# Sample attention on four column groups of the array, stacked rotary parts, head splits on ScalarE and GpSimd

## The chip, the core and the metric

The kernel runs on one core of a Trainium2 chip. The metric is the device time of one launch in microseconds. Engines are TensorE (PE; its weight loads are shown apart as PEld), VectorE (DVE), ScalarE (ACT), GpSimd (POOL) and SyncE (SP), which here only issues transfers.

## What is computed

One inference step of a decoder layer for a prompt of 512 tokens and a sample group of 8 sequences with 4 new tokens each. The part that the change touches is multi-head latent attention with 8 heads. In the prompt each head has its own keys (128 latent dimensions and 64 rotary ones shared by all heads). The sample attends to 2048 past positions in a paged cache of latent rows and to its own new tokens; its queries are absorbed into the latent space first, so all 8 heads and 4 tokens of a sequence make 32 query columns against one set of latent rows:

```python
s_past = einsum('bqhr,bkr->bhqk', q_abs, past_c) + einsum('bqhd,bkd->bhqk', q_pe, past_pe)
s_new  = einsum('bqhr,bkr->bhqk', q_abs, kv_c) + einsum('bqhd,bkd->bhqk', q_pe, k_pe)
s = concatenate([s_past, s_new], -1) * MLA_SCALE
p = softmax(where(visible, s, -inf))
o = einsum('bhqk,bkr->bqhr', p[..., :P], past_c) + einsum('bhqk,bkr->bqhr', p[..., P:], kv_c)
```

Around it stand the input projection, a gated MLP, the output projection, attention to a memory and a squared-ReLU MLP.

## The kernel before

The kernel is written engine by engine, with counting semaphores; nothing reorders it. Weights come as a stream of units of 512 KB through four raw buffers (RAW). ScalarE makes the high part of a unit (w_hi), GpSimd the low part (w_lo, line 344), and TensorE uses both: a product in split precision is three passes (PASSES: high-high, high-low, low-high) in float32r. The parts of the sample are plain float32.

The stage of the change is a loop of 8 rounds (TensorE lines 1393 to 1449). Round h does head h of the prompt and sequence b = h of the sample. TensorE's order in a round:

1. scores of the sample, four quarters of 512 positions: each two products with 128 rows (L1406) and one with the 64 rotary rows (L1407), all into partitions 0 to 31 of two PSUM banks in turn; ScalarE copies a quarter to SBUF (quarter_out, L520), VectorE takes its maximum (quarter_max, L945);
2. scores of the new keys (L1410, L1411);
3. transposes of the prompt's probabilities (L1416), then the values of the prompt (L1426), which wait for the split of these probabilities (L536 on ScalarE, L983 on VectorE);
4. seventeen small transposes of the sample's probabilities (L1431 to L1435), after an exponential over 2080 columns on 32 partitions (L539);
5. values of the sample, 16 pages and the new rows (L1440, L1441);
6. scores of the prompt's next head (head_scores, L1386 with 128 rows, L1389 with 64 rotary rows);
7. the sample's latent output turned into columns (L1447), stored by VectorE (L1000).

VectorE also splits the next head's queries, rotary queries, keys and values (stage_qk, L902 and L906; stage_v, L911 and L912) and adds the squares of the head's output (L996, L997). GpSimd is idle from the weight splits before the loop to those after it.

SyncE, in each round: read 16 page numbers into registers (L309), issue 16 transfers of page columns (L317, 192 KB each, into KT[0] to KT[3], each quarter free after its scores, kt_used), then, when the sample's values of the round before are done (pvs), 16 of page rows (L323, 128 KB each, into NAT). KT[2] and KT[3] lie over raw weight buffers. After the loop it loads weight units again.

Of the kernel before, what the change touches and what calls it, by code (L numbers as in the profile page):

```python
# [25 lines left out]
P = 128  # L26
# [9 lines left out]
QUART = PAGES // 4  # L36
MEM, MH = 256, 4
# [43 lines left out]
N_CONST = C_NEW + NB * NS  # L81
# [22 lines left out]
def trunk(nc, w_stream, x_t, mem_t, gains, consts, w_sp_t, w_sp_4, b_sp, w_uk_t, w_uv_p, pool_t, pool_n,  # L104
          pages, mem_k_t, mem_v_p, y_t, kv_t, pe_t, mk_t, mv_p, cv_t):
    with ExitStack() as ctx:
# [20 lines left out]
        def sem(name):  # L127
# [8 lines left out]
        ACCA = place("head_square_sum", [P, TOK], F32, ARENA + 13312)  # L136
        S_AT = at_end[0]
        RX = fixed("rstd_x", [P, TOK])
        TMP = [fixed(f"square{s}", [P, TOK]) for s in range(2)]
        ACC = fixed("square_sum", [P, TOK])  # L140

        S = place("sample_scores", [NS, PAST + NS], F32, S_AT)
        assert S_AT + (PAST + NS) * 4 <= at_end[0]
# [4 lines left out]
        PES = fixed("k_rope_sample", [ROPE, NS])  # L148
        KNAT = fixed("latent_sample_rows", [NS, RT * 128])
# [5 lines left out]
        QR = fixed("q_rope_batch", [ROPE, NS])  # L155
        SMX = fixed("sample_quarter_max", [NS, 8])
        SM = fixed("sample_max", [NS, 1])
        SB = fixed("sample_bias", [NS, 1])
        SS = fixed("sample_sum", [NS, 1])
        SR = fixed("sample_rsum", [NS, 1])  # L160
        PNT = fixed("new_probs_t", [NS, NS])
# [31 lines left out]

        KT = [place(f"page_cols{q}", [P, QUART, 384], F32, at)
              for q, at in enumerate((TB, TB + 6144, ARENA, ARENA + 6144))]
        QH = place("q_head_split", [P, 2, NP], F32R, TB + 12288)
        QRH = place("q_rope_head_split", [P, 2, NP], F32R, TB + 16384)
        KH = place("k_head_split", [P, 2, NP], F32R, TB + 20480)
        VH = place("v_head_split", [P, 2, 4, 128], F32R, TB + 24576)
        NAT = place("page_rows", [P, PAGES, 256], F32, TB + 28672)  # L200
        PTH = []
        off = 45056
# [3 lines left out]
        PST = place("sample_probs_t", [P, PAGES, NS], F32, TB + 56320)  # L206
        SO = place("sample_latent_rows", [NS, RT * 128], F32, ARENA + 12288)
# [26 lines left out]
        def first_bank(g):  # L234
# [11 lines left out]
        ld_kt = [sem(f"loaded_page_cols{q}") for q in range(4)]  # L246
# [15 lines left out]
        stg_qk, stg_v, sc, nb, ex, pn = [  # L262
            sem(n) for n in ("head_qk_staged head_v_staged head_scored head_bias_ready head_exp "
                             "head_probs_ready").split()]
        pt, pt_hi, pt_lo, pv, h_out = [sem(n) for n in "probs_t probs_t_hi probs_t_lo head_valued head_out".split()]
        qst, kt_used, s_max, s_out, sn, s_bias, sex, s_t, pst, pvs, s_rows, s_cols, ol = [
            sem(n) for n in ("sample_q_staged quarter_scored quarter_max quarter_out new_keys_scored "
                             "sample_bias_ready sample_exp sample_probs_transposed sample_probs_t_ready sample_valued "
# [20 lines left out]
        def _(sp):  # L289
# [47 lines left out]
        @block.gpsimd  # L337
        def _(pool):
            pool.sem_inc(w_lo, 4)

            with pool.Fori(0, UNITS // 4) as i:
                for s in range(4):
                    pool.wait_ge(w_hi, i * 4 + (s + 1))
                    nc.gpsimd.tensor_tensor(HL[s % 2][:, 1, :, :], RAW[:, s, :, :], HL[s % 2][:, 0, :, :].bitcast(F32),  # L344
                                            ALU.subtract).then_inc(w_lo, 1)

        @block.scalar
        def _(act):
            act.sem_inc(fsq, 1)
            act.sem_inc(pst, 1)  # L350
# [160 lines left out]

            act.wait_ge(c_n, 8)
            with act.Fori(0, HEADS // 2) as i:
                for hp in range(2):
                    h = i * 2 + hp

                    def quarter_out(q):

                        act.wait_ge(kt_used, h * 4 + (q + 5))
                        nc.scalar.copy(S[:, 512 * q:512 * q + 512], PSUM[0:NS, 4 + q % 2, :]).then_inc(s_out, 1)  # L520

                    quarter_out(0)
                    act.wait_ge(nb, h + 1)
                    for qb in range(4):
# [1225 lines left out]
```

## Time and profile before

| | |
|---|---|
| runs | 2740.46, 2752.51 and 2753.41 us |
| median | 2752.51 us |
| span of the profiled execution, first to last instruction | 2727.6 us |
| TensorE matmuls busy | 2575.2 us, 94% |
| weight loads | 2402.3 us, 88% |
| VectorE, ScalarE, GpSimd busy | 34%, 23%, 34% |
| mean granted TensorE clock | 0.975 |
| attention loop (first sample scores to last latent columns) | 497.3 to 764.7 us |

Times in the rows are from the start of the span, in us. An engine's busy time counts its instructions, not its waits; register instructions of SyncE are not counted. Matmul ends are modelled, so starts are the better measure. The time around the span is not in the profile.

### The profile page before, as it was taken

The page shows a single profiled execution, that of the slowest core. Times are in us where ns is not written, and L with a number is a line of the kernel's source. Part 1 is how long each engine was busy: PE and PEld are TensorE (multiplying, and loading weights), DVE is VectorE, ACT ScalarE, POOL GpSimd, SP SyncE. Part 2 cuts the span into 40 slices and gives each one's busy share as a digit, 9 for nine tenths or more (in the row PEclk, how much of TensorE's full clock was granted, in tenths as well). Part 3 has the DMA queues.
Part 4 walks back from the last instruction along what each step waited for, and adds up shares of the span by engine and source line. Part 5 has one row for each costly group of instructions (what it writes and reads, how often), then busy time and mean ns, then how long its engine had stood idle before and what let it go on. Part 6 is the DMA issues. An engine that isn't in the chain of part 4 may idle for free.

```text
span 2727.6 us, 48074 instructions
## 1 busy us (share of the span) xinstructions
PE 2575.2 (94%) x19084; PEld 2402.3 (88%) x19084; DVE 937.0 (34%) x1260; ACT 633.8 (23%) x855; POOL 919.2 (34%) x380
## 2 busy tenths in 40 slices
PE   7999878999989996999999999999999999999996
PEld 7999867444479995899999999999999999999996
DVE  5200497555443344652122131131131221221356
ACT  5111431222221132132122121121221221221221
POOL 2433432000014441233433434344343433434342
PEclk9999989899989998999999999999999999999998
DMA  5222232455432224122222222222222222222222
GB/s 220 85 85 92 93 121 70 146 155 170 145 133 87 85 78 154 40 77 92 85 86 91 85 92 85 89 88 85 92 85 91 86 86 91 85 92 85 88 89 88
DMA packets 100269, 270.68 MB, mean 99 GB/s; under 512 B 11810, under 2 KB 48707, under 8 KB 99075
## 3 DMA queue, kind: packets, MB, share of 16 engines
q1 hardware_dynamic: 92160, 243.57, 26.8%
q10 hardware_dynamic: 8066, 26.53, 2.6%
q8 instruction: 29, 0.48, 0.1%
q14 instruction: 14, 0.11, 0.0%
HBM read 263.72 MB, written 6.33 MB: 99 GB/s over the span
## 4 chain that ended last, share of the span: by engine, by line
PE 59%; issue 29%; POOL 8%; DVE 3%; ACT 1%; ACTq 0%; POOLq 0%; DVEq 0%
PE psum L1200 58%; POOL hl L344 8%; DVE square L1040 1%; DVE square_sum L1042 1%; DVE x L1037 0%; PE psum L1523 0%; DVE x L1187 0%; ACTq L603 0%; PE psum L1564 0%; ACT mem_probs L621 0%; PE psum L1502 0%; DVE mem_probs L1115 0%; PE psum L1537 0%; DVE head_max L1100 0%; DVE rstd_x L703 0%
## 5 line engine op out<-in xcount | busy, mean ns | idle before, releaser
L344 POOL TENSOR_TENSOR hl<-raw,hl 128x1024 fp32r<-128x1024 f32 x376 | 919.0, 2445 | 1777.5 <-ACT hl L651 913.1
L1200 PE MATMUL psum<-xg,hl 128*128 128x272 f32 x10272 | 1301.4, 289 | 33.5 <-DVE xg L698 20.3
L1200 PEld LDWEIGHTS psum<-xg,hl 128*128 128x128 f32 x10272 | 1297.5, 190 | 36.4 <-POOL hl L344 22.4
L1200 PE MATMUL psum<-ffn_hidden,hl 128*128 128x272 f32 x6144 | 765.9, 287 | 0.0
L1200 PEld LDWEIGHTS psum<-ffn_hidden,hl 128*128 128x128 f32 x6144 | 765.1, 188 | 0.0
L651 ACT CAST hl<-raw 128x1024 fp32r<-128x1024 f32 x254 | 267.7, 1054 | 1209.0 <-PE psum L1200 1209.0
L1175 DVE TENSOR_TENSOR x<-x,psum 128x544 f32 x112 | 80.9, 722 | 561.1 <-PE psum L1200 561.1
L1160 DVE SCALAR_TENSOR_TENSOR square<-psum,rstd_x 128x544 f32<-128x544 f32 x64 | 46.4, 725 | 486.2 <-PE psum L1200 486.2
L1164 DVE TENSOR_SCALAR ffn_hidden<-square 128x544 f32 x64 | 132.4, 2069 | 60.9 <-ACT square L660 60.9
L373 ACT CAST hl<-raw 128x1024 fp32r<-128x1024 f32 x64 | 67.4, 1053 | 318.6 <-PE psum L1200 318.6
L366 ACT CAST hl<-raw 128x1024 fp32r<-128x1024 f32 x58 | 60.6, 1048 | 188.6 <-PE psum L1200 136.6
L1042 DVE TENSOR_TENSOR square_sum<-square_sum,square 128x544 f32<-128x544 f32 x48 | 99.2, 2066 | 1.7
L1037 DVE TENSOR_TENSOR x<-x,psum 128x544 f32 x48 | 34.6, 722 | 151.7 <-PE psum L1200 144.0
L736 DVE TENSOR_TENSOR z<-psum,rstd_x 128x544 f32 x18 | 13.1, 725 | 199.7 <-PE psum L1200 199.7
L1440 PE MATMUL psum<-page_rows,sample_probs_t 128*32 128x256 f32 x256 | 65.1, 419 | 6.6 <-ACT new_probs_t L543 6.6
L1440 PEld LDWEIGHTS psum<-page_rows,sample_probs_t 128*32 128x32 f32 x256 | 30.2, 120 | 38.7 <-issue 17.6
L1406 PE MATMUL psum<-page_cols,q_abs_batch 128*32 128x512 f32 x128 | 62.6, 613 | 0.0
L520 ACT COPY sample_scores<-psum 32x512 f32<-32x512 f32 x32 | 18.4, 575 | 165.8 <-PE psum L1407 165.8
L1200 PE MATMUL psum<-mem_out_split,hl 128*128 128x272 f32 x384 | 50.9, 294 | 2.8 <-DVE mem_out_split L1143 1.9
L1200 PEld LDWEIGHTS psum<-mem_out_split,hl 128*128 128x128 f32 x384 | 49.8, 194 | 3.8 <-issue 3.8
L1166 DVE TENSOR_TENSOR ffn_hidden<-square,ffn_hidden 128x544 f32 x64 | 46.4, 726 | 12.8 <-DVE ffn_hidden L1164 7.6
L1406 PEld LDWEIGHTS psum<-page_cols,q_abs_batch 128*32 128x32 f32 x128 | 11.6, 110 | 42.4 <-issue 42.1
(218 smaller groups left out, 1344.7 us busy)
## 6 DMA issues: line engine op xcount, KB each, us to landing
raw<-in_w_stream SPq DMA_DIRECT2D x376, 512.0 KB, 3.3
page_cols<-in_pool_t SPq DMA_DIRECT2D x128, 192.0 KB, 3.6
page_rows<-in_pool_n SPq DMA_DIRECT2D x128, 128.0 KB, 2.4
x<-in_x_t ACTq DMA_DIRECT2D x4, 1088.0 KB, 12.3
out<-x SPq DMA_DIRECT2D x8, 544.0 KB, 2.7
cache_k_sb<-in_mem_k_t ACTq DMA_DIRECT2D x4, 1024.0 KB, 13.2
cache_v_sb<-in_mem_v_p ACTq DMA_DIRECT2D x1, 4096.0 KB, 19.2
x<-in_x_t ACTq DMA_DIRECT2D x1, 4080.0 KB, 14.1
```

The lines of the kernel that those rows point to most:

```text
L344: nc.gpsimd.tensor_tensor(HL[s % 2][:, 1, :, :], RAW[:, s, :, :], HL[s % 2][:, 0, :, :].bitcast(F32), ALU.subtract).then_inc(w_lo, 1)
L366: nc.scalar.copy(HL[n % 2][:, 0, :, :], RAW[:, n % 4, :, :]).then_inc(w_hi, 1)
L373: nc.scalar.copy(HL[n % 2][:, 0, :, :], RAW[:, n % 4, :, :]).then_inc(w_hi, 1)
L651: nc.scalar.copy(HL[n % 2][:, 0, :, :], RAW[:, n % 4, :, :]).then_inc(w_hi, 1)
L1042: step(tt(a0, a0, t0, ALU.add))
L1160: stt(two(TMP[0][:, :]), banks(g), 0.0, two(RX[:, :]), ALU.max, ALU.mult).then_inc(t_out, 1)
L1164: ts(hh, hs, 1.0, None, ALU.mult).then_inc(h_parts, 1)
L1166: tt(H[:, 1, bass.ds(p * 2 + t, 1), :], hs, hh.bitcast(F32), ALU.subtract).then_inc(h_parts, 1)
L1175: tt(xs, xs, banks(g), ALU.add).then_inc(t_out, 1)
L1200: last = mm(PSUM[:, s + half, 0:HALF], HL[slot][:, wp, blk, :], src[:, xp, k, HALF * half:HALF * (half + 1)], start=start and n == 0, stop ...
L1406: mm(dst, QA[:, r, :], KT[q][:, :, 128 * r:128 * r + 128], start=r == 0, stop=False)
L1440: mm(PSUM[0:NS, 7, 0:256], PST[:, g, :], NAT[:, g, :], start=g == 0, stop=False)
```

## The change

- Page columns KT become one buffer with 320 columns a page (128 + 128 latent, and the 64 rotary dimensions of two halves of 64 positions on 128 partitions) instead of 384; page rows NAT now lie over the raw weight buffers.
- The sample's scores go to one PSUM bank: quarter q on partitions 32q to 32q+31, so each quarter is a column group of the array; the rotary part is two products per quarter with 128 rows, of which 64 meet zeros. Softmax is done on 128 partitions at once with one exponential (S4), the new keys apart (SN). The probabilities are turned by four full transposes. Values are four products per group. Quarters are added when the output is turned into columns, by a matrix C_SUM4 in place of the identity, and division by the sum comes last (latent_out).
- Rotary queries are stacked: high part of one half and low part of the other on 128 rows (QRT against the high keys, QRZ against the low), five products per block in place of six.
- Splits: high parts on ScalarE (stage_qk_hi, stage_v_hi), low parts on GpSimd (stage_qk_lo, stage_v_lo). ScalarE copies the head's output and squares it, GpSimd adds the squares.
- Order on TensorE: scores of the sample, new keys, transposes of sample and prompt, values of the sample, scores of the next head, values of the prompt, columns. The scores of a ninth head are no longer computed.
- All loops over heads are written out; SyncE reads page numbers at constant places.

```diff
-            with sp.Fori(0, NB) as b:
-                pages_of = [sp.value_load(PTAB[0:1, bass.ds(b * PAGES + g, 1)], min_val=0,
+            for b in range(NB):
+                pages_of = [sp.value_load(PTAB[0:1, b * PAGES + g:b * PAGES + g + 1], min_val=0,
                                           max_val=pool_n.shape[0] - 1) for g in range(PAGES)]
-                for q in range(4):
-                    sp.wait_ge(kt_used, b * 4 + (q + 1))
-                    if q == 2:
-                        sp.wait_ge(w_lo, U_OUT + 2 + 4)
-                    for g in range(QUART):
-                        sp.dma_start(KT[q][:, g, :], pool_t[bass.ds(pages_of[QUART * q + g], 1), :, :]
-                                     .rearrange("a p n -> (a p) n")).then_inc(ld_kt[q], 16)
-                sp.wait_ge(w_used, U_KV)
-                sp.wait_ge(pvs, b + 1)
+                if b:
+                    sp.wait_ge(kt_used, b)
+                for g in range(PAGES):
+                    sp.dma_start(KT[:, g, :], pool_t[bass.ds(pages_of[g], 1), :, :]
+                                 .rearrange("a p n -> (a p) n")).then_inc(ld_kt, 16)
+                if b:
+                    sp.wait_ge(pvs, b)
+                else:
+                    sp.wait_ge(w_lo, U_OUT + 2 + 4)
                 for g in range(PAGES):
                     sp.dma_start(NAT[:, g, :], pool_n[bass.ds(pages_of[g], 1), :, :]
                                  .rearrange("a p n -> (a p) n")).then_inc(ld_nat, 16)
-            sp.wait_ge(kt_used, 4 * NB + 4)
+            sp.wait_ge(pvs, NB)
             load_unit(U_OUT + 2, 2, U_OUT + 3)
-            sp.wait_ge(s_cols, NB)
-            sp.wait_ge(stat_sum, STAT_NO["a"] + 1)
             load_unit(U_OUT + 3, 3, U_OUT + 4)
...
+            def stage_qk_lo(h):
+                pool.wait_ge(qk_hi, h + 1)
+                for dst, src in ((QH, Q[:, h, 0:NP]), (KH, KK[:, h, :])):
+                    last = nc.gpsimd.tensor_tensor(dst[:, 1, :], src, dst[:, 0, :].bitcast(F32), ALU.subtract)
+                last.then_inc(stg_qk, 1)
+            def stage_v_lo(h):
+                pool.wait_ge(v_hi, h + 1)
+                nc.gpsimd.tensor_tensor(VH[:, 1, :, :], VV[:, :, 128 * h:128 * h + 128],
+                                        VH[:, 0, :, :].bitcast(F32), ALU.subtract).then_inc(stg_v, 1)
+            stage_qk_lo(0)
+            stage_v_lo(0)
+            for h in range(HEADS):
+                if h + 1 < HEADS:
+                    stage_qk_lo(h + 1)
+                pool.wait_ge(h_out, h + 1)
...
+                    nc.gpsimd.tensor_tensor(ACCA[:, 0:NP], ACCA[:, 0:NP], HSQ[:, :], ALU.add).then_inc(hsum, 1)
...
+                if h + 1 < HEADS:
+                    stage_v_lo(h + 1)
...
+            for h in range(HEADS):
+                if h + 1 < HEADS:
+                    stage_qk_hi(h + 1)
+                if h:
+                    act.wait_ge(pv, h)
+                    nc.scalar.copy(Q[:, h - 1, 0:NP], PSUM[:, 6, :])
+                    if h > 1:
+                        act.wait_ge(hsum, h - 1)
+                    nc.scalar.activation(HSQ[:, :], PSUM[:, 6, :], ACT.Square).then_inc(h_out, 1)
+                    stage_v_hi(h)
+                act.wait_ge(nb, h + 1)
...
+                act.wait_ge(s_bias, h + 1)
+                nc.scalar.activation(S4[:, :], PSUM[:, 4, :], ACT.Exp, bias=SB[:, :], scale=MLA_SCALE,
+                                     accum_out=SS[:, :])
+                nc.scalar.activation(SN[:, :], SN[:, :], ACT.Exp, bias=SB[0:NS, :], scale=MLA_SCALE,
+                                     accum_out=SSN[:, :]).then_inc(sex, 1)
+                act.wait_ge(s_t, h + 1)
+                nc.scalar.copy(PNT[0:NS, :], PSUM[0:NS, 7, 448:448 + NS])
+                nc.scalar.copy(PST[:, :, :], PSUM[:, 5, :].rearrange("p (g q) -> p g q", g=QUART)).then_inc(pst, 1)
...
+                dve.wait_ge(kt_used, h + 1)
+                step(nc.vector.reduce_max(SMQ[:, :], PSUM[:, 4, :], AX))
+                for q in range(4):
+                    nc.vector.tensor_copy(SMX[:, q:q + 1], SMQ[NS * q:NS * q + NS, :])
+                dve.wait_ge(sn, h + 1)
+                step(tt(SN[:, :], PSUM[0:NS, 7, 256:256 + NS], C[0:NS, C_NEW + NS * h:C_NEW + NS * h + NS], ALU.add))
+                step(nc.vector.reduce_max(SMX[:, 4:5], SN[:, :], AX))
+                step(nc.vector.reduce_max(SM[:, :], SMX[:, 0:5], AX))
+                for q in range(4):
+                    last = ts(SB[NS * q:NS * q + NS, :], SM[:, :], -MLA_SCALE, None, ALU.mult)
+                last.then_inc(s_bias, 1)
...
+            for h in range(HEADS):
+                pe.wait_ge(qst, h + 1)
+                pe.wait_ge(ld_kt, (h + 1) * (16 * PAGES))
+                for r in range(RT):
                     for q in range(4):
+                        mm(PSUM[NS * q:NS * q + NS, 4, :], QA[:, r, :],
+                           KT[:, QUART * q:QUART * q + QUART, 128 * r:128 * r + 128], start=r == 0, stop=False)
+                for half in range(2):
+                    for q in range(4):
+                        dst = PSUM[NS * q:NS * q + NS, 4, :].rearrange("p (g k) -> p g k", g=QUART)
+                        last = mm(dst[:, :, 64 * half:64 * half + 64], QR[:, half, :],
+                                  KT[:, QUART * q:QUART * q + QUART, 256:PAGE_W], start=False, stop=half == 1)
+                last.then_inc(kt_used, 1)
...
+                pe.wait_ge(pst, h + 1)
+                pe.wait_ge(ld_nat, (h + 1) * (16 * PAGES))
+                for g in range(QUART):
+                    for q in range(4):
+                        mm(PSUM[NS * q:NS * q + NS, 7, 0:256], PST[:, g, NS * q:NS * q + NS],
+                           NAT[:, QUART * q + g, :], start=g == 0, stop=g == QUART - 1 and q > 0)
+                mm(PSUM[0:NS, 7, 0:256], PNT[:, :], KNAT[:, :], start=False, stop=True).then_inc(pvs, 1)
+                pe.wait_ge(pt_lo, h * 4 + 4)
+                if h + 1 < HEADS:
+                    head_scores(h + 1)
...
+                pe.wait_ge(stg_v, h + 1)
...
+                last.then_inc(pv, 1)
+                pe.wait_ge(s_rows, h + 1)
+                pe.wait_ge(s_sum, h + 1)
+                for r in range(RT):
+                    mm(PSUM[:, 7, 320 + 32 * r:352 + 32 * r], SO[:, 128 * r:128 * r + 128],
+                       C[:, C_SUM4:C_SUM4 + NS], start=True, stop=True)
...
```

## Rows read from the trace of the kernel before

**Rows 1.** Stretches table: us, busy PE, PEld, DVE, ACT, POOL; clock, DMA share, GB/s.

```profile
592.00:623.00 31.00, 28.85 (x129) 13.54 (x128) 15.90 (x43) 9.67 (x21) 0.00 (x0) 1.00 0.53 164
```

**Rows 2.** Timeline of one head, TensorE: start, us, engine, line, tiles, count.

```profile
593.03 0.62 PE L1386 MATMUL psum<-k_head_split,q_head_split 128*128 128x256 f32 x3
...
598.45 0.63 PE L1447 MATMUL psum<-consts_sb,sample_latent_rows 32*128 32x32 f32 x4
...
599.00 1.90 PE L1406 MATMUL psum<-page_cols,q_abs_batch 128*32 128x512 f32 x4
...
599.46 0.11 PEld L1406 LDWEIGHTS psum<-page_cols,q_abs_batch 128*32 128x32 f32 x1 [0.32 <-issue]
...
599.88 0.11 PEld L1406 LDWEIGHTS psum<-page_cols,q_abs_batch 128*32 128x32 f32 x1 [0.32 <-issue]
...
610.23 0.31 PE L1410 MATMUL psum<-latent_sample,q_abs_batch 128*32 128x32 f32 x4
...
610.64 1.31 PE L1416 MATMUL psum<-consts_sb,probs 128*128 128x128 f32 x10
...
613.29 2.18 PE L1426 MATMUL psum<-probs_t,v_head_split 128*128 128x512 f32 x12 [1.33 <-DVE probs_t L983]
...
617.58 7.09 PE L1440 MATMUL psum<-page_rows,sample_probs_t 128*32 128x256 f32 x32 [0.82 <-ACT new_probs_t L543]
...
625.14 0.62 PE L1386 MATMUL psum<-k_head_split,q_head_split 128*128 128x256 f32 x3
```

**Rows 3.** SyncE: transfers in the timeline, reads by line (ns), landing, waits.

```profile
593.27 8.08 SPq L323 DMA_DIRECT2D page_rows<-in_pool_n  x16
...
612.33 8.35 SPq L317 DMA_DIRECT2D page_cols<-in_pool_t  x16
...
L309 SPq FUSED_REGOPS  x248: 46/152/173, 452.6 to 709.8; - x124
...
L309 SPq TENSOR_LOAD <-page_ids x128: 261/263/463, 452.1 to 709.6; - x128
...
page_cols<-in_pool_t SPq DMA_DIRECT2D x128, 192.0 KB, 3.6
...
SPq L323 <- PE psum L1441: 32.1, 7, 6.1
```

**Rows 4.** Timeline of the same head, VectorE and ScalarE.

```profile
602.52 0.67 DVE L945 TENSOR_REDUCE sample_quarter_max<-sample_scores 32x1 f32<-32x512 f32 x1 [0.18 <-ACT sample_scores L520]
...
603.76 0.68 ACT L526 ACTIVATE probs<-psum,head_bias 128x512 f32<-128x512 f32 x1
...
604.33 0.20 ACT L526 ACTIVATION_READ_ACCUMULATOR probs<-psum,head_bias 128x1 f32 x1
...
611.55 0.17 DVE L972 TENSOR_TENSOR sample_scores<-psum,consts_sb 32x32 f32<-32x32 f32 x1
...
612.47 1.67 DVE L983 TENSOR_TENSOR probs_t<-psum,probs_t 128x512 fp32r<-128x512 f32 x4
```

**Rows 5.** Splits on GpSimd, and an addition on VectorE (by group, in the timeline).

```profile
L344 POOL TENSOR_TENSOR hl<-raw,hl 128x1024 fp32r<-128x1024 f32 x376 | 919.0, 2445 | 1777.5 <-ACT hl L651 913.1
...
L1042 DVE TENSOR_TENSOR square_sum<-square_sum,square 128x544 f32<-128x544 f32 x48 | 99.2, 2066 | 1.7
...
594.43 0.69 DVE L997 TENSOR_TENSOR head_square_sum<-head_square_sum,probs 128x512 f32<-128x512 f32 x1
```

**Rows 6.** Timeline ahead of the loop.

```profile
487.91 1.01 PE L1386 MATMUL psum<-k_head_split,q_head_split 128*128 128x256 f32 x3 [1.75 <-DVE q_abs_sample L925]
...
489.45 4.69 POOL L344 TENSOR_TENSOR hl<-raw,hl 128x1024 fp32r<-128x1024 f32 x2 [16.48 <-ACT hl L366]
...
497.32 3.62 PE L1406 MATMUL psum<-page_cols,q_abs_batch 128*32 128x512 f32 x4
```

**Rows 7.** Timeline of the last head.

```profile
749.37 8.78 PE L1440 MATMUL psum<-page_rows,sample_probs_t 128*32 128x256 f32 x32 [0.82 <-ACT new_probs_t L543]
...
764.02 0.63 PE L1447 MATMUL psum<-consts_sb,sample_latent_rows 32*128 32x32 f32 x4
```

More of the change, by code:

```diff
@@ L36 @@
 QUART = PAGES // 4
+PAGE_W = 320
 MEM, MH = 256, 4
@@ L80 @@
 C_NEW = C_BLOCK + NS
-N_CONST = C_NEW + NB * NS
+C_SUM4 = C_NEW + NB * NS
+N_CONST = C_SUM4 + NS
 class Chain:
@@ L192, in trunk @@
         PR = place("probs", [P, 1280], F32, TB + 96320)
[L194 to L200, printed above, removed]
+        KT = place("page_cols", [P, PAGES, PAGE_W], F32, TB)
+        QH = place("q_head_split", [P, 2, NP], F32R, TB + 20480)
+        QRT = place("q_rope_stack", [P, NP], F32R, TB + 24576)
+        QRZ = [place(f"q_rope_hi{s}", [P, NP], F32R, TB + 26624 + 2048 * s) for s in range(2)]
+        KH = place("k_head_split", [P, 2, NP], F32R, TB + 30720)
+        VH = place("v_head_split", [P, 2, 4, 128], F32R, TB + 34816)
         PTH = []
-        off = 45056
+        off = 38912
         for kb, w in enumerate((512, 384, 256, 256)):
@@ L245, in trunk @@
         ld_w = [sem(f"loaded_unit_slot{s}") for s in range(4)]
-        ld_kt = [sem(f"loaded_page_cols{q}") for q in range(4)]
+        ld_kt = sem("loaded_page_cols")
         ld_nat = sem("loaded_page_rows")
@@ L923, in _ @@
+            for s in range(2):
+                nc.vector.memset(QRZ[s][ROPE * (1 - s):ROPE * (1 - s) + ROPE, :].bitcast(F32), 0.0)
+            stage_rope(0)
+            nc.vector.memset(QR[:, :, :], 0.0)
+            nc.vector.memset(PNT[:, :], 0.0)
+            nc.vector.memset(PTH[3][:, 0, 0:128].bitcast(F32), 0.0)
+            step(nc.vector.memset(PTH[3][:, 1, 0:128].bitcast(F32), 0.0))
             for r in range(RT):
@@ new lines, in _ @@
+            for h in range(HEADS):
+                dve.wait_ge(sc, h + 17)
+                for qb in range(4):
+                    d = PSUM[:, qb, 128 * qb:128 * qb + 128]
+                    last = tt(d, d, causal, ALU.add)
+                step(last)
+                for qb in range(4):
+                    last = nc.vector.reduce_max(HM[:, qb:qb + 1], PSUM[:, qb, 0:128 * (qb + 1)], AX)
+                step(last)
+                ts(HN[:, :], HM[:, :], -MLA_SCALE, None, ALU.mult).then_inc(nb, 1)
+                if h:
+                    latent_out(h - 1)
+                dve.wait_ge(kt_used, h + 1)
[9 more added lines that the diff above has]
+                last.then_inc(s_bias, 1)
+                dve.wait_ge(ex, h + 1)
+                step(nc.vector.reciprocal(HR[:, :], HS[:, :]))
+                for qb in range(4):
+                    p_ = PR[:, P_AT[qb]:P_AT[qb] + 128 * (qb + 1)]
+                    last = ts(p_, p_, HR[:, qb:qb + 1], None, ALU.mult)
+                last.then_inc(pn, 1)
+                dve.wait_ge(sex, h + 1)
+                step(tt(SS[0:NS, :], SS[0:NS, :], SSN[:, :], ALU.add))
+                ts(SSB[:, :], ones, SS[:, :], None, ALU.mult).then_inc(s_sum, 1)
+                if h + 1 < HEADS:
+                    stage_rope(h + 1)
+                    stage_sample(h + 1)
+                for kb in range(4):
+                    dve.wait_ge(pt_hi, h * 4 + (kb + 1))
+                    lo = 0 if kb < 3 else 128
+                    w = NP - 128 * kb
+                    tt(PTH[kb][:, 1, lo:lo + w], PSUM[:, kb, 128 * kb:NP],
+                       PTH[kb][:, 0, lo:lo + w].bitcast(F32), ALU.subtract).then_inc(pt_lo, 1)
@@ L1376, in _, with head_scores @@
             pe.wait_ge(t_out, G_KV + 16)
[L1379 to L1382 removed]
+            def head_scores(h):
+                pe.wait_ge(stg_qk, h + 1)
+                pe.wait_ge(stg_r, h + 1)
                 for qb in range(4):
                     w = max(256, 128 * (qb + 1))
+                    q = slice(128 * qb, 128 * qb + 128)
                     for n3, (qp, kp) in enumerate(PASSES):
[L1386 to L1391 removed]
```

337 lines of the change are left out of this document (133 added, 204 removed).

## The prediction

> **What bounds the kernel now.** I read the table of stretches first. In the stage that the change touches, the eight heads of attention, TensorE is busy 28.85 of 31 us, VectorE 15.9 and every other engine less [rows 1]. So the stage is a TensorE stage, and its period is read from the timeline of one head: the score products of the next head start at 593.03 and again at 625.14, so one head takes 32.11 us [rows 2]. Within it: scores of the prompt 5.42 us (593.03 to 598.45), the columns of the sample's latent output 0.55, scores of the sample against its pages 11.23 (599.00 to 610.23), the new keys 0.41, transposes of the prompt's probabilities 1.31, values of the prompt 2.18, values of the sample 7.09 and 0.5 for the new keys (617.58 to 625.14); the rest is small transposes and two waits of 1.33 and 0.82 us. The sample's scores and values are 18.8 of 32.1 us, and the weight of each of their products has 32 columns out of 128.
>
> Then I read the queue of SyncE, which no line about busy engines shows. Per head it issues 16 transfers of page rows in 8.08 us and 16 of page columns in 8.35 us. Between the end of the one (593.27 + 8.08 = 601.35) and the start of the other (612.33) lie 10.98 us, in which it reads 16 page numbers (128 reads in eight heads) [rows 3]. That is 27.4 us of work per head in strict order. Today it waits 32.1 us in 7 times for the sample's values, 4.6 us a head [rows 3], so it has slack, and little of it: 32.1 - 4.6 = 27.5.
>
> **The change part by part.**
>
> *Sample scores and values on four column groups.* The number of products does not fall: 8 of 512 columns and 8 of 256 for the scores, 16 of 256 for the values. What may fall is the time, if groups run at once. One product is two matmuls: weight loads of one product start at 599.46 and 599.88, 0.43 apart [rows 2]. A product of 256 columns takes 7.09 / 16 = 0.44. One after another the scores are 16 x 0.43 + 8 x 0.44 = 10.4 us and the values 7.0; with four at once 3.0 and 2.0. No row shows two groups side by side, so these are the bounds. I take two at once, 5.6 and 3.7 us: the two matmuls of one product go to the same group one after the other, and if matmuls start in program order, as they do in all these rows, the next group can only overlap the second of them.
> The Trainium skill says the same in "TensorE: Matmul & The Clock Gate" (The mechanism): matmuls to different tiles overlap, but start and end strictly in order. By its 2.38 times for three column tiles the scores would be an estimated 4.4 us. It changes the TensorE period below, not the period that I forecast.
>
> *Stacked rotary parts.* 24 products become 20, all with 128 rows. The 24 take 5.42 us; the 12 products of the prompt's values, which have half as many columns in all and no change of row count, take 2.18 [rows 2]. So the 8 changes of row count cost (5.42 - 4.36) / 8 = 0.13 us each, and 20 products without a change are 2.18 x 20 / 12 = 3.6 us. Bounds 3.6 and 4.5 (20/24 of 5.42).
>
> *The chain between scores and values.* It was partly covered; now nothing of the prompt's values stands in it. After the scores, VectorE reduces all partitions once (0.67) instead of four quarters, does the new keys' part and the maxima, which take 0.9 today from 611.55 to 612.47, and seven tiny operations more (0.17 at most each, overlapping: some 0.9): 2.5 us [rows 4]. ScalarE's exponential of 512 columns with its read of the sum is 0.9 (603.76 to 604.53) and that of the 32 new keys some 0.4 [rows 4]; together TensorE stands 3.8 us after the scores, with 0.4 of new keys beside it. Five full transposes instead of seventeen small ones: 5 x 0.13 = 0.65; ten for the prompt 1.3 [rows 2]. The exponential of 2080 elements on 32 partitions and three ScalarE copies of quarters go.
>
> TensorE's period: 3.6 + 2.2 (values of the prompt) + 0.8 (three products for the columns instead of two, 0.55 x 1.5) + 5.6 + 3.8 + 0.65 + 1.3 + 3.7 + 0.5 + 0.3 for handing over = 22.4 us. One after another it is 30.5, with four at once 18.1. The clock adds to this: values of the sample took 7.09 busy us in the head shown and 8.78 in the last head [rows 2, 7], after the same stretch of transposes and waits, so one fall of the clock costs 1.7 us. The new waits are longer, so I put one or two falls into each head: 24 to 26 us.
>
> *Head splits moved to ScalarE and GpSimd.* A split of 512 columns on GpSimd is half of 2.4 us [rows 5]; two for queries and keys, one for values and one addition of squares are 4.9 us a head, started early in a period of over 20. The first copies and the squares on ScalarE are some 3 us more in a queue that is busy a third of the time. On VectorE they go. VectorE operations with operands in SBUF wait for GpSimd: an addition of 544 columns took 2.07 us beside its weight splits, one of 512 took 0.69 in the loop, where GpSimd is idle [rows 5]. GpSimd's work comes in the first 6 us of a period, where VectorE does the prompt's maximum, not on the chain above. Cost: none; if that cover is gone, 1 us a head.
>
> *SyncE's queue.* The order is read numbers, columns, rows, as before, with 16 reads and 32 transfers per head. The transfers cost what they do, 8.35 + 8.08. The index of a read becomes a constant. A read has two register steps today, the shorter 0.046 us [rows 3]; with the time to issue it I estimate 0.09 us, so at best the 16 reads lose 1.4 us, and the loop's branch goes. At worst they lose nothing. So the queue needs 9.6 + 8.35 + 8.08 + 0.3 = 26.3 us a head, between 25.7 and 27.4. This is longer than TensorE's 22 to 26. All waits in the queue come true earlier than it reaches them, so the stage's period is that of the queue: **26.3 us**.
>
> *Start.* The first head's splits stand behind two weight splits on GpSimd, which end at 489.45 + 4.69 = 494.1 [rows 6], and take 2.4: TensorE starts the first scores at 496.5 instead of 487.9 and, standing idle, at the low clock (three products took 1.01 against 0.62 [rows 2, 6]). The sample's first scores start at about 501.8 instead of 497.3 [rows 6]. That is covered by the queue: page rows of head 0 are issued from 494.3 (they wait for that same weight split), until 502.4; numbers until 512.0; page columns of head 1 until 520.3, landed 3.6 later [rows 3], 523.9. TensorE would be there at about 525.
>
> *End.* The last head computes no scores for a ninth head: 5.42 us of TensorE go, 2.2 of values move there. The weight loads of the output projection start after the sample's values instead of after its scores; the units are needed 15 us later, so this costs nothing.
>
> *The sum.* Columns of head 7 have landed at 523.9 + 6 x 26.3 = 681.7. From there 5.6 + 3.8 + 0.65 + 1.3 + 4.2 + 2.2 + 0.8 = 18.6 us, with two falls of the clock 22, to the last columns of the latent output: 703.7. Before, they ended at 764.02 + 0.63 = 764.7 [rows 7]. All that follows depends on these and is the same. The gain is **61 us**. It is made against the profiled execution, whose span is 2727.6; the runs lie 13 to 26 us above that span. The median of the runs, 2752.5, gives 2691.5 (own range 2685 to 2701 by the queue's 25.7 to 27.4, six times, and 2 us at the end).
>
> **The rivals.**
> *Groups don't overlap*, so that the change does not do what it says: TensorE's 30.5 us is then the period. 8 x 1.6 = 13 us less, 3 less at the end, 4 more at the start: 2740, within 0.5%. For it: no row shows an overlap, and every product here is two full matmuls. Against: it would need different groups to wait for each other.
> *Slower: every change of column group costs what a change of row count costs*, 0.13 us. With 32 changes a head and no overlap the period is 34.7, so 8 x 2.6 + 1 = 22 us more: 2774. It decides from 0.05 us per change on, where 32 changes eat up the 1.6 us. For it: the measured price of the row changes. Against: the weight shape stays the same from group to group.
> The Trainium skill, "TensorEngine Tiling (Array Packing)" (Key Properties), says that a change of tiling mode drains the array and a change of tile alone does not. The 0.13 us agrees with its first half; on the second half no run here has spoken. By it this rival would not occur; by the first half applied to every group it is the 2774.
> *The queue is not the bound*, because reads with a constant index cost far less than today's 10.98 / 16 = 0.69 us. Then TensorE's 23 to 24 us set the period: some 20 us less than forecast, 2670. Nothing in the rows shows such a read.
>
> **How the numbers follow.** Forecast 0.66, no overlap 0.16, slower 0.10, queue cheap 0.08. Differences under 0.5% (14 us) can't be told from no change here. Faster are the forecast and the cheap queue: 0.74; same is the rival without overlap: 0.16; slower 0.10. The range reaches to the cheap queue and the case without overlap, 2668 to 2741, and leaves out about 2 in 10.
>
> **What would show it.** In the profile after: a head's period of 26 us; SyncE issuing with no wait for TensorE, and TensorE waiting some us before the sample's scores for page columns; about 9.6 us between the last page rows of one head and the first page columns of the next; starts of the sample's matmuls that overlap in pairs, scores 5 to 6 us; 20 score products in 3.6 us; values of the sample slower in many heads by the clock. A period near 30.5 with serial matmuls, or over 32, makes the forecast wrong; so does a queue that still waits.

## The result and the profile after

The changed kernel takes 2653.7 us (median; 2651.6 to 2654.7), the kernel before, run beside it, 2749.8: a ratio of 0.967, 95% interval 0.964 to 0.970, or 96 us less. The forecast was 2691.5 with a range of 2668 to 2741: faster as foretold, but 38 us lower than forecast and 14 below the range.

| us in the profiled execution | before | after | forecast |
|---|---|---|---|
| span | 2727.6 | 2652.9 | 2666.6 (61 less) |
| last columns of the latent output end | 764.7 | 693.6 | 703.7 |
| from there to the end | 1962.9 | 1959.3 | the same |
| period of a head, mean of six | 32.95 (32.1 or 33.8) | 25.8 | 26.3 |
| TensorE waits for page columns | 0 | 33.3 in 7 | some us a head |

The timeline of one head after the change, all engines (SPq is SyncE's queue; the brackets give the idle time ahead and what ended it):

```profile
558.47 2.42 PE L1474 MATMUL psum<-page_rows,sample_probs_t 128*32 128x256 f32 x28
...
560.69 8.06 SPq L324 DMA_DIRECT2D page_cols<-in_pool_t  x16
...
561.24 0.62 PE L1432 MATMUL psum<-k_head_split,q_head_split 128*128 128x256 f32 x3
...
564.55 2.11 PE L1488 MATMUL psum<-probs_t,v_head_split 128*128 128x512 f32 x12
...
568.93 8.43 SPq L332 DMA_DIRECT2D page_rows<-in_pool_n  x16
...
571.92 3.64 PE L1444 MATMUL psum<-page_cols,q_abs_batch 128*32 128x512 f32 x16 [4.67 <-DMA page_cols<-in_pool_t]
...
575.31 1.90 PE L1449 MATMUL psum<-page_cols,q_rope_batch 128*32 128x256 f32 x16
...
581.00 0.23 PE L1459 MATMUL psum<-consts_sb,sample_new_probs 32*32 32x32 f32 x1 [3.62 <-ACT sample_new_probs L595]
...
584.34 3.35 PE L1474 MATMUL psum<-page_rows,sample_probs_t 128*32 128x256 f32 x32
...
586.36 1.88 SPq L324 DMA_DIRECT2D page_cols<-in_pool_t  x4
```

From one issue of page columns to the next is 586.36 - 560.69 = 25.67 us: 8.06 and 8.43 us of issues with 0.18 between them, and from 568.93 + 8.43 = 577.36 to 586.36 the reads of 16 page numbers. TensorE reaches the sample's scores, finds the page columns not landed and waits 4.67 us. The score products that follow run at the lower of the clock's two levels (granted clock 0.50, which is 1.2 GHz, from 571.92 to 575.31): they take 3.64 us, and 1.92 where TensorE didn't wait (below). The prompt's 20 score products take 564.55 - 561.24 = 3.31 us.

The table of stretches there (columns as in [rows 1]):

```profile
550.00:575.00 25.00, 16.70 (x129) 11.47 (x121) 11.00 (x41) 8.43 (x24) 4.95 (x4) 0.77 0.60 181
```

TensorE, 28.85 of 31 us busy before, is busy 16.70 of 25, and its granted clock is 0.77 of full speed in the mean.

Who waits for whom in the eight heads, TensorE and SyncE's queue (us in all, times, longest):

```profile
PE psum L1444 <- DMA page_cols<-in_pool_t: 33.3, 7, 6.9
PE psum L1459 <- ACT sample_new_probs L595: 29.9, 8, 4.6
PE psum L1432 <- POOL k_head_split L365: 11.4, 1, 11.4
...
SPq L332 <- POOL hl L351: 25.4, 1, 25.4
SPq L302 <- PE psum L1476: 10.0, 1, 10.0
```

SyncE waits ahead of the first page rows and behind the last, and nowhere between. Its 32.1 us of waits for the sample's values [rows 3] have gone, and TensorE waits instead.

### The profile page after: what moved, and what is told of

Same layout as the page of the kernel before. It is cut to its first block, busy times and chain, and to the rows that moved or that the text cites. A ratio compares the mean times of both kernels' runs of the same rounds, so it can differ in the third digit from the quotient of the medians.

```text
span 2652.9 us, 47225 instructions
## 1 busy us (share of the span) xinstructions
PE 2447.7 (92%) x19004; PEld 2368.7 (89%) x19004; DVE 893.7 (34%) x1238; ACT 628.7 (24%) x884; POOL 957.4 (36%) x412
## 4 chain that ended last, share of the span: by engine, by line
PE 70%; issue 14%; SPq 5%; POOL 5%; DVE 5%; ACT 1%; ACTq 0%; DVEq 0%; DMA 0%; POOLq 0%
PE psum L1243 67%; POOL hl L351 5%; SPq L318 2%; SPq L324 2%; SPq L332 2%; DVE square L1085 1%; DVE square_sum L1087 1%; PE psum L1394 0%; DVE x L1082 0%; PE psum L1572 0%; DVE x L1232 0%; DVE square L812 0%; PE psum L1613 0%; ACT mem_probs L688 0%; PE psum L1551 0%
## 5 line engine op out<-in xcount | busy, mean ns | idle before, releaser
L382 POOL TENSOR_TENSOR head_square_sum<-head_square_sum,head_square 128x512 f32<-128x512 f32 x7 | 8.8, 1263 | 142.6 <-ACT head_square L581 122.1
L1444 PE MATMUL psum<-page_cols,q_abs_batch 128*32 128x512 f32 x128 | 25.1, 925 | 33.3 <-DMA page_cols<-in_pool_t 33.3
L1243 PE MATMUL psum<-q_split,hl 128*128 128x272 f32 x288 | 40.0, 304 | 4.1 <-DVE q_heads L908 2.9
L1243 PEld LDWEIGHTS psum<-q_split,hl 128*128 128x128 f32 x288 | 39.2, 203 | 5.0 <-DVE q_heads L908 3.3
L1085 DVE TENSOR_TENSOR square<-x 128x544 f32 x48 | 43.1, 897 | 1.6
```

Source lines behind the costliest of these rows:

```text
L1085: step(tt(t0, xs, xs, ALU.mult))
L1243: last = mm(PSUM[:, s + half, 0:HALF], HL[slot][:, wp, blk, :], src[:, xp, k, HALF * half:HALF * (half + 1)], start=start and n == 0, stop ...
```

## The experiments

Ratios are to the kernel before, run on the same chip. Variants of the changed kernel are compared by their medians, since each repeats within 1 to 6 us (but for the shifted one at the end). They did not all run on one chip; from the last columns to the end, where no edit but the shifts reaches, their profiled executions took 1954.5 to 1961.9 us (the changed kernel 1959.3), so differences of 2 or 3 us between variants say nothing.

**What bounds the new kernel: reads at once.** One instruction reads a head's 16 page numbers, without the steps that test their bounds (shortened):

```
-pages_of = [sp.value_load(PTAB[0:1, b * PAGES + g:b * PAGES + g + 1], min_val=0, ...) for g in range(PAGES)]
+pages_of = nc.values_load_multi_w_load_instructions(PTAB[0:1, b * PAGES:(b + 1) * PAGES], ...)[1]
```

> The 16 page numbers of a head are read by one instruction and without the two bounds steps. Theory A, SyncE's queue sets the period of 25.65 us in the changed kernel: the read stretch of 9.3 us shrinks to under 1 us, the queue then needs about 17 us a head, and TensorE's own 20.9 us (25.65 less the mean wait of 33.3 / 7 = 4.76 us for page columns) become the bound. The 33.3 us of waits go: 2653.7 - 33 = about 2620 us, and down to 2608 if the clock, which is low after the waits, recovers. Rival B, the transfers themselves set the period (the DMA engines are 0.60 busy in the loop): issued earlier they land no earlier, the waits for page columns stay, 2645 to 2654.

Measured: 2607.2 us, ratio 0.953 (0.948 to 0.958), 46 less than the changed kernel, as theory A has it with the clock recovered. The reads by line (ns, least/median/most), after and then in this run, and its first waits:

```profile
L318 SPq TENSOR_LOAD <-page_ids x128: 261/266/462, 448.1 to 662.8; - x128
L318 SPq FUSED_REGOPS  x128: 147/147/170, 448.6 to 663.1; - x128
```

```profile
L318 SPq TENSOR_LOAD <-page_ids x8: 967/974/1180, 448.1 to 616.0; - x8
...
PE psum L1460 <- ACT sample_new_probs L596: 30.0, 8, 4.6
PE psum L1433 <- POOL k_head_split L366: 11.4, 1, 11.4
```

The wait for page columns is gone, and the period is 18.7 us. More fell than the 33.3 us of waits: the sample's scores of the eight heads, 32.5 us together in the changed kernel, took 21.0. Without the waits they run at full speed, 1.74 us to the first rotary product against 3.39 above:

```profile
566.78 1.95 PE L1475 MATMUL psum<-page_rows,sample_probs_t 128*32 128x256 f32 x32
...
568.56 0.59 PE L1477 MATMUL psum<-latent_sample_rows,new_probs_t 128*32 128x256 f32 x2
...
575.02 1.92 PE L1445 MATMUL psum<-page_cols,q_abs_batch 128*32 128x512 f32 x16
...
576.76 1.05 PE L1450 MATMUL psum<-page_cols,q_rope_batch 128*32 128x256 f32 x16
...
577.62 0.29 PE L1456 MATMUL psum<-latent_sample,q_abs_batch 128*32 128x32 f32 x4
```

SyncE's queue has little room even so, since its issues of page columns got longer, 9.00 us for 16 against 8.06:

```profile
560.41 9.00 SPq L325 DMA_DIRECT2D page_cols<-in_pool_t  x16
...
560.00:580.00 20.00, 14.53 (x125) 10.91 (x125) 12.55 (x51) 8.46 (x25) 6.82 (x7) 0.91 0.81 248
```

One issue of the 16 takes 1.21 us there, where the others take 0.33; in heads 2 to 7 the longest takes 0.94 to 1.41. The DMA engines are busier over the whole stretch (0.81 instead of 0.60), but while the issues run their share is 0.83 against 0.80, so the share doesn't explain it, and the cause stays open.

**The same edit on the kernel before.**

> The same edit to the kernel before. Theory A, TensorE's 32.1 us a head bounded that kernel and the queue had 4.6 us of slack: SyncE's wait for the sample's values grows from 4.6 to about 14 us a head and the time doesn't move, 2750 within 5 us. Rival B, the queue already limited some heads of the kernel before: faster by 10 us or more.

Measured: 2744.4 us, ratio 1.003 (0.9997 to 1.006): no gain, as theory A has it. SyncE's waits for the sample's values grew from 32.1 us to 93.0 in 7, 13.3 a head, so the time that the reads gave back went into waiting. That queue bounds the kernel after and didn't bound the one before.

**What the column groups are worth.** The group becomes the outer loop, in the scores and in the values (the scores, shortened):

```
-for r in range(RT):                 +for q in range(4):
-    for q in range(4):              +    for r in range(RT):
         mm(PSUM[NS*q:NS*q+NS, 4, :], QA[:, r, :], KT[:, QUART*q:..., 128*r:...], ...)
```

> The changed kernel with the products of one column group issued one after the other (group outermost) in the sample's scores and values; same products, same result. Theory A, matmuls start in the order of the program, so that groups overlap only where neighbours in that order lie in different groups: scores 10 us instead of 2.6, values 6 to 7 instead of 1.8 to 2.7, TensorE 20.9 + 7.6 + 4.5 = 33 us a head, above the queue's 25.65, the waits for page columns go and SyncE waits instead: 2653.7 + 7 x 7.4 + 12 at the end = about 2715 us. Rival B, the four groups run at once whatever the order: 2654. Rival C, half of the overlap stays (5.6 and 3.7 us): TensorE 25.4, hidden under the queue, 2654 to 2660, and the timeline tells it from B.

Measured: 2665.4 us, 12 more than the changed kernel; scores 7.6 us, values 4.2 to 5.6. The period is 26.3 us, just above the queue's 25.8, and TensorE's waits for page columns fall to 1.6 us. The time is near theory C, although less of the overlap stays than C said, and A's premise falls. TensorE in this run:

```profile
603.70 1.90 PE L1444 MATMUL psum<-page_cols,q_abs_batch 128*32 128x512 f32 x4
605.44 0.38 PE L1448 MATMUL psum<-page_cols,q_rope_batch 128*32 128x256 f32 x1
605.45 0.62 PE L1444 MATMUL psum<-page_cols,q_abs_batch 128*32 128x512 f32 x1
605.66 0.59 PE L1448 MATMUL psum<-page_cols,q_rope_batch 128*32 128x256 f32 x2
605.90 0.59 PE L1444 MATMUL psum<-page_cols,q_abs_batch 128*32 128x512 f32 x1
```

A group has four matmuls on L1444 and then four on L1448. The second group's first (605.45) starts beside the first group's fifth (605.44), ahead of its sixth (605.66), which stands earlier in the program. So matmuls of different groups do not start in program order; within a group they do. A reading that fits and was not tested: each group has a queue of its own for a few matmuls. The Trainium skill says in "TensorE: Matmul & The Clock Gate" (The mechanism) that matmuls are strictly first in, first out; this trace differs, and the trace decides.

**The same with reads at once.**

> Page numbers read at once, and the groups issued one after the other. Theory A, TensorE sets the period of 26.3 us of the serial kernel, and taking 8 us of work from the queue changes nothing there: 2660 to 2666, so that the overlap of the groups is worth about 57 us once the queue is out of the way, where it showed as 11 us with the queue in it. Rival B, the queue was still the bound of the serial kernel: 2640 or less.

Measured: 2659.6 us against 2607.2 with the groups interleaved: 52 us, as theory A has it. With the queue in the way the same order cost 12.

**The rotary part taken apart,** with the queue in the way and without (shortened):

```
-mm(.., QRT[:, q], PEH[:, 0, 0:w]);  mm(.., QRZ[h % 2][:, q], PEH[:, 1, 0:w])
+mm(.., QRT[p, q], PEH[p, 0, 0:w]);  mm(.., QRT[p, q], PEH[p, 1, 0:w])
+mm(.., QRZ[1 - h % 2][p, q], PEH[p, 0, 0:w])            # p: 64 rows; VectorE writes the low part there
```

> The changed kernel with the rotary part of the prompt's scores as three products of 64 rows instead of two stacked ones of 128. The 24 products should take 5.4 us again instead of 3.3. Theory A, the queue sets the period: the 2.1 us lie in the wait for page columns, whose sum falls from 33.3 to about 18 us, and the time stays, 2654 within 4 us. Rival B, TensorE sets it: 8 x 2.1 = 17 us more, 2671.

> Page numbers read at once, and the rotary part as three products of 64 rows. Theory A, with the queue out of the way TensorE's 18.7 us set the period, and the 2 us that four times three products of other row count cost now show: 8 x 2 = 16 us more than with the page numbers at once alone, 2607 + 16 = 2623. Rival B, the queue (9 + 8.5 + 1.1 = 18.6 us a head) is still the bound: 2607 to 2612.

Measured: 2657.2 us with the queue in the way (the profiled span is 2653.1, that of the changed kernel 2652.9), and 2624.9 without, 18 more than 2607.2. That is theory A both times. With the queue in the way, the wait for page columns took up the cost; it was 33.3 us and is now:

```profile
PE psum L1446 <- DMA page_cols<-in_pool_t: 22.5, 6, 5.9
```

**Head splits on VectorE again** (second half of each split, heads 1 to 7; reads at once).

> Page numbers read at once, and the second half of the head splits (queries, keys, values) of heads 1 to 7 made by VectorE again instead of GpSimd. A split is 0.69 us on VectorE (an operation of 512 columns) and 1.27 on GpSimd. Theory A, VectorE has room: the two splits of queries and keys stand ahead of the prompt's last subtractions, for which TensorE's next scores wait with about 1.1 us of slack, so the period grows by 0.3 to 1 us: 2609 to 2615 against 2607 with GpSimd. Rival B, hidden wholly: 2605 to 2609, the move to GpSimd is then worth nothing. Rival C, VectorE becomes the chain: 2625 or more.

Measured: 2605.6 us against 2607.2, which can't be told apart: rival B. The move of these to GpSimd is worth nothing here.

**Filling TensorE's wait.** The prompt's values and the columns of the head before go between the sample's scores and its transposes; ScalarE's and VectorE's steps follow. In the second run GpSimd's order is changed too:

```
 for h in range(HEADS):
-    if h + 1 < HEADS: stage_qk_lo(h + 1)
+    if h + 2 < HEADS: stage_qk_lo(h + 2)      # stage_qk_lo(1) ahead of the loop
     pool.wait_ge(h_out, h + 1)
```

> Page numbers read at once, and the prompt's values and the columns of the head before put into TensorE's wait of 3.6 us between the sample's scores and its transposes. TensorE's period would fall from 18.7 to about 16. Theory A, the queue's 18.2 to 18.8 us a head take over at once: 2603 to 2607, no change that can be measured, with waits for page columns back. Rival B, the queue has room: 8 x 2.5 = 20 us less, 2587. Rival C, VectorE's and ScalarE's later steps delay the chain by more than the gap holds: slower than 2612.

> The kernel with the filled wait, with one more edit: GpSimd makes the query and key splits of the head after next before it waits for the squares of the head before, instead of behind that wait. In the run without it TensorE stood 3.1 to 4.7 us before the prompt's scores, six times 23.1 us in all, for a key split that GpSimd had queued behind its wait for ScalarE, and the scores behind it ran at the low clock (5.9 us instead of 3.3). Theory A, that order was the whole reason: TensorE's period falls from 22.25 to about 17, the queue's 18.2 to 18.8 take over, 2603 to 2609. Rival B, the longer way through VectorE and ScalarE was part of it: 2612 to 2620. Rival C, the queue has room and the filled wait pays: 2590.

Measured: 2623.0 and 2608.9 us. The first is rival C, by another way than it said: GpSimd's queue, in strict order, held the next key split behind a wait for ScalarE's squares, and TensorE stood, 23.1 us in six heads. The timeline of one of them:

```profile
573.70 1.28 POOL L383 TENSOR_TENSOR head_square_sum<-head_square_sum,head_square 128x512 f32<-128x512 f32 x1 [16.80 <-ACT head_square L605]
...
576.18 1.26 POOL L366 TENSOR_TENSOR q_head_split<-q_heads,q_head_split 128x512 fp32r<-128x512 f32 x1
577.40 1.26 POOL L366 TENSOR_TENSOR k_head_split<-k_heads,k_head_split 128x512 fp32r<-128x512 f32 x1
578.76 0.98 PE L1433 MATMUL psum<-k_head_split,q_head_split 128*128 128x256 f32 x3 [3.14 <-issue]
```

With the order changed the time is that of reads at once, not 20 us less, since SyncE's queue (18.7 us a head) takes over and TensorE waits for page columns again:

```profile
PE psum L1467 <- DMA page_cols<-in_pool_t: 12.0, 6, 3.2
```

**Sharing the issues.** ScalarE issues four of the 16 transfers of page rows.

> The kernel with the filled wait and GpSimd's new order, in which TensorE waits for page columns again, with one more edit: of the 16 transfers of page rows of heads 1 to 7, ScalarE issues four, with their page numbers, and SyncE twelve. The same bytes move. Theory A, issuing is what limits SyncE's queue: 4 x 0.52 = 2.1 us leave it, the waits for page columns (12.0 us in 6) go, the period falls from 18.7 to about 17.2 and the time from 2609 by 7 x 1.5 = 10 to about 2598. Rival B, the DMA engines' throughput limits it (0.85 busy, 252 GB/s): issues take longer by as much as they get fewer, 2605 to 2610. Rival C, the four issues stand ahead of ScalarE's splits of the next head and delay the chain: 2612 or more.

Measured: 2602.3 us, ratio 0.949 (0.945 to 0.953), the least of all and 6.6 less than without the edit; in the profiled executions 3.5 us of that are in the heads (last columns at 644.0 for 647.5). This is between A and B: the waits for page columns are gone, SyncE waits again,

```profile
SPq L333 <- PE psum L1515: 14.5, 7, 3.2
...
560.00:580.00 20.00, 16.62 (x135) 11.46 (x134) 13.13 (x48) 9.58 (x30) 5.05 (x4) 0.91 0.86 260
580.00:600.00 20.00, 16.62 (x125) 11.01 (x125) 12.55 (x44) 8.69 (x25) 5.07 (x4) 0.83 0.81 246
```

and the period is 18.3 us, TensorE's own, with a granted clock of 0.83 to 0.91. So issuing was the limit, and little lies behind it.

**Why the median of before misled: the same kernel once more, and two shifts in SBUF.**

> The kernel before, unchanged, with another profiled execution. Theory A, the runs of this kernel differ among themselves by what the clock does in the sample's values (6.7 or 8.4 us a head, so up to 8 x 1.7 = 13.5 us) and in the stages behind: the time lies within 2720 to 2755, 1.8 us above its own span, and heads of 32.1 and of 33.8 us alternate in another mixture than the 32.95 us mean of the first profile. Rival B, 13 to 26 us lie around the span in every execution, as the prediction took it: a span near 2727 with a time near 2750.

Measured: the profiled execution took 2751.8 us with a span of 2750.0, so 1.8 us lie around the span, as in every execution on record whose span is known: theory A, B falls. But the clock in the heads, which A named first, doesn't make the 22 us between this span and 2727.6: the heads took 1.9 us longer and started 1.8 earlier, and both executions end the last columns at 764.7. Most of it, 20 us, is in the feed-forward stage (1530.8 and 1551.2 us from its first product to its last), which no edit touches; the granted clock is 1.00 there in both. Mean distance of the starts of its products of 272 columns, worked out from the traces:

| us | input projections (100 to 300) | feed-forward (1280 to 2580) | all runs |
|---|---|---|---|
| before | 0.1261 | 0.1244 | 2740 to 2753, with later runs 2722 to 2754 |
| before again | 0.1250 | 0.1261 | 2728 to 2752 |
| before, shifted | 0.1244 | 0.1244 | 2722 to 2731 |
| after | 0.1244 | 0.1244 | 2652 to 2655 |
| after, shifted | 0.1261 | 0.1256 | 2656 to 2681 |

The change makes some small tiles larger and so moves the region of the activations (TB) from byte 72000 of a partition to 72288. The shifts add unused bytes and nothing else:

```
+fixed("pad", [P, 72])     # before: TB at 72288, as in the changed kernel;  in the changed kernel [P, 56]: TB at 72512
 TB = at_end[0]
```

> The kernel before with 288 unused bytes put ahead of the large region in SBUF that holds the activations, so that this region begins where it begins in the changed kernel (byte 72288 of a partition instead of 72000). No instruction changes. In the three profiled executions of the kernel before, a product of 272 columns in the weight-streaming stages starts every 0.1244, 0.1250, 0.1256 or 0.1261 us, one value for each stage of an execution; in all of the changed kernel and its variants it is 0.1244. 16416 such products times 0.0017 us are 28 us. Theory A, the address sets it: with the region shifted every stage runs at 0.1244 and all runs lie near the lowest of before, 2718 to 2728, within 3 us of each other. Rival B, it hangs on something else that changed, such as the loops of the queues: 2721 to 2753 as before, spread and all.

> The changed kernel with 224 unused bytes at the same place, so that the region begins at byte 72512, on a multiple of 64 as in the kernel before, where the changed kernel has it at 72288, 32 bytes beside one. Theory A, the address sets the rhythm: stages at 0.1250 to 0.1261 us appear, the runs spread over 2655 to 2682. Rival B, it is something else: 2652 to 2656.

Measured: before, shifted, 2727.8 us, ratio 0.9945 (0.9925 to 0.9966); after, shifted, 2674.4 us, 21 more than unshifted. Theory A both ways, although the shifted kernel before spreads over 9 us and not 3. The same 6144 products of the feed-forward stage (busy us, mean ns) in before again, before shifted, after, and after shifted:

```profile
L1200 PE MATMUL psum<-ffn_hidden,hl 128*128 128x272 f32 x6144 | 776.1, 288 | 0.0
```

```profile
L1201 PE MATMUL psum<-ffn_hidden,hl 128*128 128x272 f32 x6144 | 765.9, 287 | 0.0
```

```profile
L1243 PE MATMUL psum<-ffn_hidden,hl 128*128 128x272 f32 x6144 | 765.9, 287 | 0.0
```

```profile
L1244 PE MATMUL psum<-ffn_hidden,hl 128*128 128x272 f32 x6144 | 772.7, 288 | 0.0
```

The kernel before ran beside each group of experiments, with medians from 2733.7 to 2749.8, and the 96 us are against the highest of them. They part into 6 of such chance (2749.8 - 2743.4), some 16 of the address (2743.4 - 2727.8) and 2727.8 - 2653.7 = 74 of the rest of the change. In the profiled executions 69 of these 74 are there by the last columns of the attention stage (762.4 us before, shifted, and 693.6 after). Which property of the address counts was not tried; of those seen, 72000 and 72512 are multiples of 64 and 72288 isn't.

## Why the prediction was right or wrong

- **The bound moves to SyncE's queue: right.** Reads at once moved the changed kernel by 46 us and the kernel before by nothing. The period was mis-sized by 0.5 us (25.8 for 26.3): the reads take 9.0 us, not 9.6, and of the 0.3 for the rest 0.18 is there. A read got 0.09 us shorter, as estimated (start to start 0.547 for 0.636); the other 0.6 us are mostly the loop's branch, which the sum named and gave no number (0.47 us before the first read, 601.35 to 601.82).
- **Two groups at once: wrong, and by luck it cost the forecast little.** The step that failed is "if matmuls start in program order, as they do in all these rows, the next group can only overlap the second of them". Scores took 2.6 us where the clock was up (575.02 to 577.62 with reads at once), not 5.6, and the values 1.8 (566.78 to 568.56), not 3.7: four at once, a quarter of the serial sums (10.4 / 4 and 7.0 / 4) and less than the text's own lower bounds of 3.0 and 2.0. The forecast went by the queue, which hid it in seven heads; it shows in the end, below. With the queue shortened, TensorE's period is 18.7, near the 18.1 that the text gave for four at once without falls of the clock; its rival "queue not the bound" used 23 to 24.
- **Stacked rotary parts: right.** 3.31 us for a forecast of 3.6; taken apart 5.4, as before. The price of a change of row count comes out higher, (5.4 - 24 x 3.31 / 20) / 8 = 0.18 us for 0.13.
- **The chain from scores to transposes: right,** 4.0 us for 3.8 (3.62 idle and 0.4 of new keys). The clock falls, put at one or two a head, are there: scores 3.64 for 1.92 after the wait for columns, and after the chain the transposes, 3.34 us for 1.95 (581.00 to 584.34, granted clock 0.50), and values.
- **Splits hidden: right,** and worth nothing either (2605.6 with VectorE). A GpSimd split took 1.26 us for 1.2. The "1 us a head" without cover was right too: with the filled wait and GpSimd's new order, a split runs beside VectorE's bias of the prompt's maximum, which took 1.09 to 1.15 us in seven heads instead of 0.17.
- **Start: 3 us early.** TensorE's first scores started at 493.84 for a forecast of 496.5, since the input projections ran at the faster rate: in the shifted changed kernel, where they ran at 0.1261, they started at 496.80. Page columns of head 1 had landed by 520.8 for 523.9 (shifted, 523.9).
- **End: 17.9 us for 22.** From the landing of head 7's columns (675.7) to the end of the last columns (693.6). Here the two groups at once entered the sum, 5.6 us for the scores and 4.2 for the values with the new keys. They took 4.4 (675.73 to 680.13) and 3.35 (687.45 to 690.80), although the clock was low in part of both (granted 0.58 and 0.67). At full speed they would be 2.6 and 2.3, 4.9 us less than the sum had. The falls of the clock came, and cost some 4 us for the 3.4 allowed.
- **The base of the sum: wrong, and the largest term.** The step is "the runs lie 13 to 26 us above that span", which took a difference between executions for time around one, and set a gain read from one execution against the median of others. The runs showed that 1.8 us lie around a span, and that executions of this kernel differ by up to 32 us (2722 to 2754); between the two profiled ones 20 of 22 us lie in the rate of one stage. The median that was used, 2752.5 of three executions, lay near the upper end of this. From that profiled execution (2727.6 + 1.8 = 2729.4) the same 61 us give 2668.4; this is 23.1 of the 37.8 us of the miss. Of the rest, 10.1 us are the start, six periods and the end (693.6 for 703.7), 3.6 the stages behind (some 2 of these by the faster rate: the output projections started 1872 products every 0.1245 us for 0.1256), and 1.0 the profiled execution's 2654.7 us against the median.
- **"All that follows is the same": wrong** by the tile addresses. The larger tiles are in the change; no row of before could say that an address sets a rate, but two rates for the same products stood in its trace (0.1261 and 0.1244), and the runs' spread of 13 us asked for them.
- **The rivals.** "No overlap" and "a change of group costs 0.13 us" fell with the group timing. "Queue not the bound" is wrong for this kernel, although 2670 lay nearer the time than the forecast did.

## What to carry to other kernels

Add up what a queue issues in a period before believing in a bound by engine: 16 reads of 0.55 us and 32 issues of 0.52 us set the time of a stage whose busiest engine was 67% busy (16.70 of 25 us). What a saving is worth shows only once the next bound is out of the way: 12 or 52 us for the same overlap. And before setting a gain against a median, find out in which stages executions of the old kernel differ, and look whether the change moves addresses of tiles that it doesn't otherwise touch.

## What the runs showed of the hardware

- The start address of the SBUF region that holds the streamed operand decides whether TensorE's weight-streaming stages hold their rate. At byte 72288 every trace shows 0.1244 us a product; at 72000 and 72512 a whole stage runs at 0.1244, 0.1250, 0.1256 or 0.1261, and in the next execution at another of them. It is up to 20 us in the feed-forward stage alone.
- Four column groups of 32 run fully beside each other: their 16 matmuls of 512 columns take 1.74 us, where one group's four took 1.74 alone (603.70 to 605.44), and one group's matmul can start ahead of another's that stands earlier in the program (605.45 and 605.66).
- Reading one page number costs SyncE 0.55 us (0.27 the load, 0.15 the bounds, the rest between); sixteen in one instruction 0.97.
- Issuing a transfer with an address from a register costs SyncE 0.52 us (16 in 8.06); with reads at once most sets of 16 page columns hold one issue of 0.94 to 1.41 us (16 in 9.00), at nearly the same DMA share while they run (0.83 for 0.80).
- A VectorE operation of 4 columns, the bias of the prompt's maximum, took 1.15 us in the one head of the changed kernel where a GpSimd split ran beside it (at 502.08), and 0.17 in the other seven.
